# A two-layer hybrid block: where VectorE works off the multiply-adds of the modulation rows

## The reference

```python
mod = jax.nn.silu(c) @ w_mod[l] + b_mod[l]              # 6 rows of 1024: shifts, scales and gates
sh1, sc1, ga1, sh2, sc2, ga2 = jnp.split(mod, 6)
modc = jax.nn.silu(c_ctx) @ w_mod[l] + b_mod[l]         # the same for the context tokens
h = rms_norm(x, norm1_g[l]) * (1 + sc1) + sh1
# four mixers on h @ w_in[l]: A mLSTM, B global attention, C window attention with sinks,
# D neighbourhood attention; each ends in softmax(q k^T / 8) v for B, C and D
y = sum_i sigmoid(gate_i) * (branch_i @ w_branch[i]);  x = x + ga1 * (y @ w_out[l])
# then rms_norm with sc2, sh2; mixture of 32 experts, 2 per token; x = x + ga2 * f
```

## Time and profile before

| | |
|---|---|
| median of 3 runs | 2814.11 us (2812.05 to 2814.51) |
| the profiled execution | 2816.22 us, of which the span from first to last instruction is 2814.7 us |
| TensorE busy | 2516.1 us (89%) |
| VectorE busy | 1036.4 us (37%) |
| ScalarE busy | 491.4 us (17%) |
| mean granted clock of TensorE | 0.945 |
| stage B, C of layer 0 | about 555 to 735 us and 735 to 900 us of the span |
| stage B, C of layer 1 | about 1985 to 2090 us and 2090 to 2180 us of the span |

### The profile page before, as it was taken

How to read it: one execution, slowest core, us unless ns; L and a number is a source line. 1 busy time by engine, 2 the same in 40 slices (tenths; PEclk the granted TensorE clock), 3 DMA queues, 4 the chain that set the end, 5 groups by cost and what they waited for, 6 DMA issues and landing times.

```text
span 2814.7 us, 45297 instructions
## 1 busy us (share of the span) xinstructions
PE 2516.1 (89%) x18928; PEld 1540.4 (55%) x18929; DVE 1036.4 (37%) x2408; ACT 491.4 (17%) x978; POOL 246.3 (9%) x406
## 2 busy tenths in 40 slices
PE   7999989999889959999999989999999758878774
PEld 3455545454444457777777545567666434444442
DVE  1226536266464322222222340536456422111112
ACT  2023222222221101111111021323222101110110
POOL 3000000000000011111111100000000021111111
PEclk9999989999999959999999988999999879999998
DMA  9181112133325429999999842123455749999994
GB/s 286 60 358 60 45 47 64 47 131 99 94 96 146 167 100 372 373 372 379 384 374 388 294 129 90 60 94 98 157 176 147 259 193 409 412 414 413 412 400 162
DMA packets 153682, 616.64 MB, mean 219 GB/s; under 512 B 17649, under 2 KB 22065, under 8 KB 137009
## 3 DMA queue, kind: packets, MB, share of 16 engines
q1 hardware_dynamic: 126850, 557.88, 53.0%
q0 software_dynamic: 21584, 36.48, 4.7%
q10 hardware_dynamic: 5152, 20.97, 1.8%
HBM read 598.30 MB, written 46.32 MB: 229 GB/s over the span
## 4 chain that ended last, share of the span: by engine, by line
PE 69%; DMA 16%; DVE 8%; issue 5%; ACT 2%; POOL 1%; SPq 0%; DVEq 0%; POOLq 0%; ACTq 0%
DMA ring<-in_e_down_dram 14%; PE bank L1624 12%; PE bank L1372 12%; PE bank L1266 11%; PE bank L1256 6%; PE score_banks L1641 4%; PE score_banks L1661 3%; PE bank L1385 2%; PE score_banks L1646 2%; PE bank L1543 2%; PE score_banks L1421 2%; PE turned_banks L1431 2%; PE bank L1295 2%; PE bank L1607 1%; PE bank L1445 1%
## 5 line engine op out<-in xcount | busy, mean ns | idle before, releaser
L1624 PEld LDWEIGHTS bank<-scr,ring 128*64 128x64 f32 x8192 | 341.6, 138 | 14.4 <-issue 14.2
L1624 PE MATMUL bank<-scr,ring 128*64 128x96 f32 x8192 | 347.8, 247 | 1.2 <-DVE scr L2329 1.2
L1372 PE MATMUL bank<-HT,ring 128*128 128x512 f32 (+1 forms) x1024 | 343.9, 491 | 0.8 <-ACT scr L987 0.4
L1266 PE MATMUL bank<-ring,HT 128*128 128x512 f32 (+1 forms) x800 | 303.5, 536 | 0.0
L1617 PE MATMUL bank<-ring,scr 128*64 128x256 f32 x2048 | 239.0, 387 | 44.2 <-DMA ring<-in_e_up_dram 21.3
L1372 PEld LDWEIGHTS bank<-HT,ring 128*128 128x128 f32 x1024 | 190.7, 190 | 139.2 <-issue 126.9
L1266 PEld LDWEIGHTS bank<-ring,HT 128*128 128x128 f32 x800 | 151.9, 193 | 142.6 <-issue 136.5
L1617 PEld LDWEIGHTS bank<-ring,scr 128*64 128x64 f32 x2048 | 145.5, 139 | 141.0 <-DMA ring<-in_e_gate_dram 39.3
L1256 PE MATMUL bank<-HT,ring 128*128 128x512 f32 (+1 forms) x512 | 195.0, 539 | 1.8 <-ACT HT L987 1.8
L1661 PE MATMUL score_banks<-ring,scr 128*64 128x512 f32 x512 | 133.5, 669 | 41.6 <-DMA ring<-in_e_down_dram 39.9
L1256 PEld LDWEIGHTS bank<-HT,ring 128*128 128x128 f32 x512 | 96.2, 190 | 91.7 <-issue 88.5
(11 more groups left out here) (261 smaller groups left out, 2759.3 us busy)
## 6 DMA issues: line engine op xcount, KB each, us to landing
ring<-in_e_up_dram SPq DMA_DIRECT2D x64, 2048.0 KB
ring<-in_e_down_dram SPq DMA_DIRECT2D x64, 2048.0 KB
ring<-in_e_gate_dram SPq DMA_DIRECT2D x64, 2048.0 KB
ring<-in_w_in_dram SPq DMA_DIRECT2D x34, 2048.0 KB
ring<-in_w_mod_dram SPq DMA_DIRECT2D x32, 1024.0 KB, 5.3
ring<-in_w_mod_dram SPq DMA_DIRECT2D x8, 2048.0 KB
ys<-consts ACTq DMA_DIRECT2D x1, 12288.0 KB, 39.7
ys<-consts ACTq DMA_DIRECT2D x1, 8192.0 KB, 64.2
```

Of the source, the lines that this page charges most:

```text
L1266: m = pe.matmul(bank[:, 0:width], HT[:, k, t * P:t * P + P], w[:, k, 0:width], start=k == 0, stop=k == KT_D - 1)
L1372: m = pe.matmul(bank[:, 0:NQ], w[:, k, (ft % 4) * P:(ft % 4) * P + P], HT[:, k, 0:NQ], start=k == 0, stop=k == KT_D - 1)
L1624: m = pe.matmul(ps[bank][rows_, f * cap:f * cap + cap], w[:, k, f * P + hf * HALF:f * P + hf * HALF + HALF], XTv[:, k, :], start=k == 0, s ...
```

## The change

In a step of D, B or C that continues a sum (not in the first step of a sum), up to two of the step's instructions of `accumulate` are issued between `peaks(i)` and `normalise(i)`; the others stay at the step's end. With four per step this is two early and two late. In D there are no sums. Over the program that is 3 of 4 steps for each of 8 sums in layer 0 (48 instructions) and 1 of 2 steps for each of 8 sums in layer 1 (16 instructions). The instructions, their number and their order among each other stay as they are.

```diff
+                    def piece(b, i, late):
+
+                        for j in range(len(sum_blocks(l, b))):
+                            first, last = sum_span(l, b, j)
+                            ops, width = sum_list(l, b, j), last - first
+                            if not first <= i < last:
+                                continue
+                            part = ops[len(ops) * (i - first) // width:len(ops) * (i - first + 1) // width]
+                            early = 0 if i == first else min(2, len(part) // 2)
+                            part = part[early:] if late else part[:early]
+                            if part:
+                                accumulate(b, j, part)
+
                     for i in range(n + 1):
                         if i < n:
                             peaks(i)
+                            piece(b, i, 0)
                             normalise(i)
...
                         fill(b, groups[half:])
-                        for j in range(len(sum_blocks(l, b))):
-                            first, last = sum_span(l, b, j)
-                            ops, width = sum_list(l, b, j), last - first
-                            part = ops[len(ops) * (i - first) // width:len(ops) * (i - first + 1) // width] if first <= i < last else []
-                            if part:
-                                accumulate(b, j, part)
+                        piece(b, i, 1)
```

## The result

The changed kernel takes 2796.62 us in the median of 5 runs (2793.2 to 2800.67), the kernel before 2814.11 us (2811.87 to 2816.89). The ratio is 0.9941 with a 95% interval of 0.9926 to 0.9955: 17.5 us less. The forecast was 2799.8 us.

A forecast was written before the change was run, and what follows sets the result against it. TensorE's waits for VectorE's division were taken to bound stages B and C. Lead 3.9 + 6.05 + 1.33 + 1.33 = 12.6 us plus clock 1.7 makes 14.3 us, median 2799.8 us, range 2794.5 to 2806.5.

The forecast's parts named there:

- What bounds the kernel, and the gap: Stages B and C: TensorE's transposes wait for VectorE's division, ceiling 22.7 us; VectorE's idle gap under the exponentials hides two multiply-adds.
- rival e: Early multiply-adds wait for their half of `w_mod`, delaying the division; 2833 us with 2 us at each place; chance 0.04.
- (d): The gap gives no cover, or the edit does nothing of what it says: 2814 us; chance 0.06.
- the lead: TensorE's gain over before from shorter waits in B and C of both layers: 12.6 us together.
- (c): The lead is given back later, in a DMA-bound stage, in layer 0 above all: 2811.4 us; chance 0.08.
- The price of a narrow step: Narrow gaps do not hide the two multiply-adds whole: 0.27 us over in B, 0.2 us in C.
- The sum for C0: Stage C of layer 0: lead summed item by item to 6.05 us, falling back at step 6's bank wait.
- The clock: Of three low stretches in C, only the second, at layer 0's gate steps, goes: 1.7 us; the others stay.
- Layer 1: Stages B and C of layer 1 gain 1.33 us each.
- From the stages to the end: Output projection and experts start by TensorE's progress, so the whole 14.3 us is passed on to the end.
- rival (a): All three low clock stretches vanish, C of layer 0 gaining 9.9 us: sum 17.8 us, median 2796.3 us; chance 0.20.

The follow-up runs named there:

- the first trace: Profile of the changed kernel as first measured, two multiply-adds per step in the gap, against the kernel before: 2796.62 us, ratio 0.9941.
- the second: The changed kernel run again unaltered, with another trace: 2796.63 us, ratio to the kernel before 0.9934.

## Why the prediction was right

*What bounds the kernel, and the gap.* Right. TensorE's waits fell from 4.7 to 0.6 us in B0 (0.8 was forecast) and from 18.2 to 13.1 in C0 (12.1), where part of the clock's gain may have turned into waiting, and nothing was seen of the other mechanisms: no wait for a half of `w_mod` (rival e), exponentials as before (d), and the lead kept to the end (c).

*The price of a narrow step.* Too high: taken as 0.27 in B and 0.2 us in C, measured 0.07 us in C (1.41 less 1.34) and 0.15 in B:

```profile
654.33 0.17 DVE L2146 TENSOR_SCALAR nms<-nm 128x2 f32<-128x2 f32 x1
654.41 1.41 DVE L2005 SCALAR_TENSOR_TENSOR scr<-ring,csil,scr 128x512 f32<-128x512 f32 x2
655.74 0.16 DVE L2158 RECIPROCAL rden<-rsum 128x2 f32<-128x2 f32 x1
```

1.41 us from the scaling to the reciprocal here, against the instruction's 0.17 and the idle 1.09 before. I let the multiply-adds start after the small instruction had ended; they start 0.08 us after its start. With 0.15 in place of 0.27 the same sum gives 4.2 for B0, and 4.3 was measured.

*The sum for C0.* Forecast 6.05 for the lead and 1.7 for the clock, 7.75; measured 10.5 and 9.9. I let VectorE's lead fall to TensorE's at item 6, where before VectorE waited for a bank. That wait came with the low stretch: it is there (0.2 to 1.0 us) in six of the seven traces with a low stretch behind item 5's wait, and in none of the five without one; without it the step gives 1.2 us like the others. This is the term that was mis-sized: 7.7 us of lead and 2.8 of clock instead of 6.05 and 1.7.

*The clock.* Its place was half right. I kept the low stretch at item 5 because the wait stayed 2.93 us; it went in the first trace and was there for a step in the second. That a wait decides by its length alone, as I reasoned, does not hold: the long waits mostly have a stretch behind them (six of seven at item 5), but of the shorter ones in B0 one of 1.65 us had one behind it and one of 1.88 had none. The Trainium skill (TensorE: Matmul & The Clock Gate, section on the HAM clock gate) says of the moment at which activity releases the clock that it differs from run to run. The traces agree with it in kind: the same kernel's C0 step at item 6 takes 5.9 us in one trace and 7.5 in the other.

*Layer 1.* B1 1.1 us (1.33 forecast). C1 0.2 and 1.5 us (1.33 forecast): in the first trace the longer low stretch, 0.66 over 10 us, took back what the lead gave.

*From the stages to the end.* The stages give 16.1 to 16.8 us, forecast 14.3; the medians differ by 17.5 us. The two profiled executions differ by 19.8 us of span. From the last scores of C1 to the end it is 653.4 us in the trace of before, 649.7 and 649.2 in the two of the changed kernel, and between 647.0 and 653.1 in the others, shorter on the whole in the faster kernels. I did not look for the cause; it stays open whether this is more than the spread of the experts, which wait for their weights' DMAs. So a part of how near the number came is luck: it lies at rival (a)'s 2796.3 us, and in C0 what (a) says did happen (9.9 us there, 10.5 and 9.9 measured), but in C1 the low stretch stayed, where (a) lets it vanish, and what is missing there was made up outside the four stages, which no term of the prediction names.

## What to carry to other kernels

If an engine issues in order and sits idle for a partner's result at every step, put independent work of at most that length ahead of the wait, not behind it: here it cost at most 0.15 us there, and the step ended earlier. Count what the moved work itself waits for, because everything behind it waits too (VectorE stood idle for 6.83 us in one step here). And when TensorE's waits are shortened, read its clock in the same stretch; a wait that VectorE's chain forces can be filled with matrix work if the clock is to stay (only transposes of the identity were tried here).

## What was not expected of the hardware

A VectorE instruction that does not wait for the small one of 0.16 us ahead of it starts 0.08 us after that one's start (753.18 and 753.26 us for lines 2144 and 2005), while one that waits for it through a semaphore starts 0.20 us after it (754.59 and 754.78 for lines 2157 and 2158). And 64 additional VectorE instructions beside ScalarE's exponentials lengthened neither: the exponentials' median is 676 against 677 ns, and the additional instructions take 743 to 753 ns each, line 2005 in the trace of before 739 to 753.
